# Latent attention: rows scaled before they are turned, and query and key heads made as features by tokens

## The chip, the cores and the metric

The kernel runs on one core of one Trainium2 chip. The metric is the device time of one execution in microseconds (us), measured over three runs; one more execution is profiled. The engines go by the profile's names: PE is TensorE's matmul, PEld its weight load, DVE VectorE, ACT ScalarE, POOL GpSimd, SP the engine that issues the loads of weights.

## What is computed

Two stacks of transformer blocks over 256 tokens with 1024 features, two layers each. The part that the change touches is the latent attention of the first stack, once a layer:

```python
def rmsnorm(x, g):
    y = xf * lax.rsqrt(jnp.mean(xf * xf, axis=-1, keepdims=True) + EPS)
    return (y * g.astype(jnp.float32)).astype(x.dtype)

# z = rmsnorm(x) @ w_in; c_q (256 x 384), c_kv (256 x 256), k_rope (256 x 64) are columns of z
def mla_attention(c_q, c_kv, k_rope, positions, norm_q, norm_kv, w_uq, w_ukv):
    q = (rmsnorm(c_q, norm_q) @ w_uq).reshape(bsz, seq, MLA_HEADS, QK_NOPE + QK_ROPE)
    kv = (rmsnorm(c_kv, norm_kv) @ w_ukv).reshape(bsz, seq, MLA_HEADS, QK_NOPE + V_DIM)
    q_nope, q_pe = q[..., :QK_NOPE], q[..., QK_NOPE:]
    k_nope, v = kv[..., :QK_NOPE], kv[..., QK_NOPE:]
    q_pe = apply_rope(q_pe, cos[:, :, None, :], sin[:, :, None, :])
    k_pe = apply_rope(k_rope, cos, sin)
    ...
        logits = (jnp.einsum('bqhd,bkhd->bhqk', qn, k_nope) + jnp.einsum('bqhr,bkr->bhqk', qp, k_pe)) * scale
        p = jax.nn.softmax(jnp.where(causal, logits, NEG_INF), axis=-1)
        return jnp.einsum('bhqk,bkhd->bqhd', p.astype(v.dtype), v)
```

There are 4 heads; QK_NOPE and V_DIM are 128, QK_ROPE is 64. The scores need queries and keys with the features on the partitions, the values with the tokens there.

## The kernel before

Tokens are two tiles (TT) of 128 rows, and a product contracts 128 features at a time on the partitions. Every weight product is made in three parts, from an upper and a lower half of each operand: `three` (line 517) multiplies upper by upper, upper by lower and lower by upper into one PSUM sum. In it a 128 x 128 tile of the activations is the stationary side and 512 (or 256) columns of weights the moving side, so the result has tokens on the partitions.

Weights stream through a ring of four chunks that SP loads (line 494). For each half chunk ACT makes the upper half (`cut`, line 2254) and DVE the lower one (line 1386). A cut may be made once PE has done with the half that lay in its slot; `half_used` tells that. Each engine has its own row of instructions, in the order of the program text of its function; semaphores alone tie them. PSUM has eight banks of 128 x 512; `free` and `held` make PE wait until a bank has been emptied.

The order in a layer around the change:

1. `project_in`: twelve blocks of z = h @ w_in, of which block 11 holds the latent columns c_q and c_kv (at Z_CQ and Z_CKV). ACT takes the squares of their rows behind block 4. Through the blocks DVE computes the 31 taps of a convolution (line 1721), the last of them in block 6; PE's matmuls of `mean` (line 844), in the last quarter of block 6, wait for tap 30.
2. `nsa_attention`: the latent rows are turned on PE in five tiles (`parts`, `part_group`, line 658: four tiles at once, one later) and cut into halves with the norm's weights (`c_hi`, `c_lo`). Then eight units of the sparse attention run in a loop: scores (952), softmax on DVE and ACT, transposes of the weights (693), ACT's copy (2399), values (709), DVE's gated output (1878) and POOL's sum over branches (2967). Between units stand other pieces: behind unit 1 DVE computes the mean squares of the latent rows, from which POOL makes the norm factors (`root`, line 2953); behind unit 4 PE makes the query product `uqn` (banks 0 and 1), behind unit 6 `uqp`. DVE scales these results by the norm factor as it empties them (1863).
3. `latent_attention`: PE makes `ukv`, key and value halves together, two halves of weights after each other. Behind the first half it turns the sparse attention's output (`nsaT`, line 658). ACT scales keys and values as it empties them (2370). PE turns the query heads (`qnT`) and starts the branch product `nsa0`; behind its first half it turns the key heads (`knT`) and then the rows that POOL has rotated (`rotT`, `kpT`; POOL's lines 2971 to 2987). Each turned pair of heads is copied from PSUM by DVE or ACT.
4. The latent attention's two units follow, among the rest of the branch products.

In the trace `ps` is PSUM, `z` the projections, `tT` and `nT` buffers of turned tiles, `ostage` the sparse attention's output, `st` the norm factors, `ring`, `upper_w` and `ring_lo` the weights with their two halves, `const` the identity for transposes. A helper's line stands for every caller.

## Time and profile before

| | us |
|---|---|
| median of three runs | 2070.93 |
| lowest, highest | 2070.07, 2073.01 |
| profiled execution, its own time | 2073.56 |
| its span, from first to last instruction | 2072.1 |
| PE busy in the span | 2044.6 |
| DVE busy | 1431.9 |
| ACT busy | 1180.3 |
| POOL busy | 65.8 |

Busy is the time in which an engine had at least one instruction under way. Matmuls overlap, so the duration of one matmul says little; the distance between the starts of two neighbours is what one costs. Where a row of the timeline stands for several instructions, its second column is the time from the first start to the last end. Idle time of an engine other than the one that bounds a stretch costs nothing by itself.

### The profile page before, as it was taken

To read this page: it belongs to the slowest core of one execution; us is meant where nothing else is said; L and a number is where in the kernel's file an instruction comes from. 1 tells how busy PE (TensorE), PEld (TensorE's weight loads), DVE (VectorE), ACT (ScalarE), POOL (GpSimd) and SP (SyncE) were. 2 spreads that over 40 slices of the span, in tenths; PEclk is the share of its full clock that TensorE was granted. 3 is DMA by queue.
4 is the path that set the end of the run, shared out by engine and by line. 5 is a ranking of instruction groups with operands and counts; after the bars stand their busy time and mean duration, and the time that the engine had idled before them with its cause. 6 is when DMAs were issued, how large, how long until landed. Compare 5 with 4: busy or idle time off the path is not lost.

```text
span 2072.1 us, 27212 instructions
## 1 busy us (share of the span) xinstructions
PE 2044.6 (99%) x10690; PEld 1723.7 (83%) x10690; DVE 1431.9 (69%) x2056; ACT 1180.3 (57%) x1906; POOL 65.8 (3%) x101
## 2 busy tenths in 40 slices
PE   9999999999999999999999999999999999999998
PEld 7877888888887788888888888878888888887887
DVE  6987756764698875676577557776765766587763
ACT  5547566553546656555465457755554655486552
POOL 0001100000000200000000000000000000010000
PEclk9999999999999999999999999999999999999999
DMA  7572344555555244455455554515555555545553
GB/s 251 198 247 100 144 164 149 191 196 183 186 202 213 92 163 158 154 198 183 183 203 193 185 212 183 214 68 195 185 184 200 186 192 186 203 151 192 186 199 123
DMA packets 54902, 372.56 MB, mean 180 GB/s; under 512 B 7471, under 2 KB 7767, under 8 KB 11128
## 3 DMA queue, kind: packets, MB, share of 16 engines
q1 hardware_dynamic: 49392, 356.54, 47.5%
q10 hardware_dynamic: 4872, 12.70, 1.9%
q0 software_dynamic: 512, 1.57, 0.3%
q8 instruction: 86, 1.41, 0.3%
q14 instruction: 40, 0.33, 0.0%
HBM read 369.46 MB, written 1.34 MB: 179 GB/s over the span
## 4 chain that ended last, share of the span: by engine, by line
PE 92%; ACT 3%; DVE 3%; DMA 1%; issue 1%; POOL 0%; SPq 0%; DVEq 0%; ACTq 0%; POOLq 0%
PE ps L567 21%; PE ps L519 17%; PE ps L523 17%; PE ps L520 17%; PE ps L573 11%; PE ps L709 1%; DMA ring<-in_w 1%; PE ps L602 1%; PE ps L642 1%; PE ps L658 1%; PE ps L693 1%; DVE ring_lo L1386 1%; ACT S L2392 1%; ACT upper_w L2254 0%; PE ps L1207 0%
## 5 line engine op out<-in xcount | busy, mean ns | idle before, releaser
L1386 DVE TENSOR_TENSOR ring_lo<-ring,upper_w 128x1024 fp32r<-128x1024 f32 x435 | 525.4, 1222 | 202.7 <-ACT upper_w L2254 201.6
L2254 ACT CAST upper_w<-ring 128x1024 fp32r<-128x1024 f32 x435 | 449.3, 1050 | 277.6 <-DMA ring<-in_w 163.3
L520 PE MATMUL ps<-ring_lo,nT_pair 128*128 128x512 f32 (+1 forms) x984 | 382.2, 388 | 0.0
L519 PE MATMUL ps<-upper_w,nT_pair 128*128 128x512 f32 (+1 forms) x848 | 337.4, 398 | 2.2 <-DVE ring_lo L1386 1.5
L523 PE MATMUL ps<-upper_w,nT_pair 128*128 128x512 f32 (+1 forms) x680 | 265.4, 390 | 0.0
L573 PEld LDWEIGHTS ps<-nT_pair,ring_lo 128*128 128x128 f32 x1920 | 246.2, 191 | 9.4
L573 PE MATMUL ps<-nT_pair,ring_lo 128*128 128x256 f32 x1920 | 249.0, 283 | 0.0
L520 PE MATMUL ps<-ring_lo,z_hi 128*128 128x512 f32 x624 | 242.9, 389 | 0.0
L567 PE MATMUL ps<-nT_pair,upper_w 128*128 128x512 f32 x960 | 230.0, 391 | 0.0
L520 PEld LDWEIGHTS ps<-ring_lo,nT_pair 128*128 128x128 f32 x984 | 185.6, 189 | 35.3
L567 PEld LDWEIGHTS ps<-nT_pair,upper_w 128*128 128x128 f32 x960 | 176.5, 188 | 34.2
L523 PE MATMUL ps<-upper_w,tT_lo 128*128 128x512 f32 (+1 forms) x528 | 204.8, 388 | 0.0
L519 PEld LDWEIGHTS ps<-upper_w,nT_pair 128*128 128x128 f32 x848 | 159.9, 189 | 38.6 <-issue 3.5
L1386 DVE TENSOR_TENSOR ring_lo<-ring,PT_w 128x1024 fp32r<-128x1024 f32 x112 | 134.9, 1220 | 55.2 <-ACT PT_w L2254 55.2
L1386 DVE TENSOR_TENSOR ring_lo<-ring,S_w 128x1024 fp32r<-128x1024 f32 x112 | 134.7, 1219 | 46.5 <-ACT S_w L2254 46.5
L2254 ACT CAST PT_w<-ring 128x1024 fp32r<-128x1024 f32 x112 | 115.5, 1050 | 70.0 <-DMA ring<-in_w 70.0
L2456 ACT COPY z<-ps 128x512 f32<-128x512 f32 x60 | 35.2, 587 | 207.6 <-PE ps L573 207.6
L523 PEld LDWEIGHTS ps<-upper_w,nT_pair 128*128 128x128 f32 x680 | 127.9, 188 | 27.3 <-DVE nT_pair L1448 0.7
L1618 DVE TENSOR_TENSOR acc<-ps,z 128x512 f32<-128x512 f32 x60 | 41.5, 692 | 156.0 <-ACT z L2456 156.0
L2254 ACT CAST S_w<-ring 128x1024 fp32r<-128x1024 f32 x112 | 115.5, 1050 | 55.8 <-DMA ring<-in_w 55.6
L519 PE MATMUL ps<-upper_w,z_hi 128*128 128x512 f32 x360 | 142.1, 395 | 0.0
L520 PEld LDWEIGHTS ps<-ring_lo,z_hi 128*128 128x128 f32 x624 | 117.3, 188 | 23.4
(389 smaller groups left out, 2876.7 us busy)
## 6 DMA issues: line engine op xcount, KB each, us to landing
ring<-in_w SPq DMA_DIRECT2D x338, 1024.0 KB, 4.8
big<-in_gains ACTq DMA_DIRECT2D x7, 512.0 KB, 4.2
z<-in_mem ACTq DMA_DIRECT2D x2, 1024.0 KB, 7.5
big<-skew POOLq DMA_DIRECT2D x8, 192.0 KB, 6.7
x<-in_x SPq DMA_DIRECT2D x2, 512.0 KB, 7.4
ring<-in_w SPq DMA_DIRECT2D x2, 512.0 KB, 7.0
PTs<-skew ACTq DMA_DIRECT2D x1, 1024.0 KB, 4.6
big<-skew ACTq DMA_DIRECT2D x1, 1024.0 KB, 8.8
```

The costliest lines, as they stand in the source:

```text
L519: PE.matmul(out, hi, w_hi, start=start, stop=False)
L520: PE.matmul(out, hi, w_lo, start=False, stop=False)
L523: return PE.matmul(out, lo, w_hi, start=False, stop=stop)
L567: PE.matmul(ps[:, base + i, :], upper(W.halves[h][2])[:, cols], nT_pair[:, :, 2 * c + k, :], start=(c == 0 and k == 0), stop=False)
L573: m = PE.matmul(ps[:, base + i, 0:T], w_lo[:, cols], nT_hi[:, 2 * c + k, :], start=False, stop=(2 * c + k == KT - 1))
L602: m = PE.transpose(ps[:, b, i * P:(i + 1) * P], src[:, t, (4 * g + i) * P:(4 * g + i + 1) * P], ident)
L642: m = PE.transpose(ps[:, b, (i * TT + t) * P:(i * TT + t + 1) * P], src(c + i, t), ident)
L658: m = PE.transpose(ps[:, b, (i * TT + t) * P:(i * TT + t + 1) * P], src(c + i, t), ident)
L1386: V.tensor_tensor(ring_lo[:, q % RING, cols], ring[:, q % RING, cols], upper(n).bitcast(F32), ALU.subtract).then_inc(*lo_cut.up(h))
L1618: V.tensor_tensor(pair(b), ps[:, base:base + 2, 0:T], ffn_half[:, 0:2, :], ALU.add).then_inc(*dve_out.up())
L2254: A.copy(upper(n), ring[:, q % RING, part * HALF:(part + 1) * HALF]).then_inc(*hi_cut.up(h))
L2456: A.copy(ffn_half[:, 0:2, :], ps[:, base:base + 2, T:2 * T]).then_inc(*act_out.up(f"{f}.hg{b}"))
```

## The change

The mean squares of the latent rows move from the loop of the sparse attention into block 6 of `project_in`. POOL, once it has both norm factors, multiplies the latent columns of z by them in place, in four instructions, and PE's turns of these columns wait for that. The gains of the norm stay where they were, in the cut behind the turn.

A new helper `three_turned` exchanges the sides of the three products: 128 columns of weights are stationary, and the 256 tokens of a turned tile are the moving side, so the result has the features of one head on the partitions. The query product `uqn` and the key half of `ukv` are made so, head by head, each over all of its row blocks; both halves of the weights are awaited before the first matmul. Their results are copied once, without a factor, into the places that the turned heads had. The turns `qnT` and `knT` go. The value half of `ukv` is made as before, behind the key half, and the turn `nsaT` stands behind the first half of the value product. Values and rotary queries are copied without a factor.

```diff
...
+        def three_turned(out, hi, lo, w_hi, w_lo, start, stop):
+            PE.matmul(out, w_hi, hi, start=start, stop=False)
+            PE.matmul(out, w_hi, lo, start=False, stop=False)
+            return PE.matmul(out, w_lo, hi, start=False, stop=stop)
         def gemm(seg, lhs, banks, ready=(), beside=None, first=0, kts=None, width=BLK):
...
         def nsa_attention(l):
-            c_at = parts(f"{l}.c", cols_of(z, Z_CQ), 4, lambda c: (), (6, 7))
+            c_at = parts(f"{l}.c", cols_of(z, Z_CQ), 4, lambda c: [pool_out.at(f"{l}.latents")], (6, 7))
...
-            beside = {4: lambda: latent_queries(f"{l}.uqn", 512, (0, 1), f"{l}.qn"), 6: lambda: latent_queries(f"{l}.uqp", 256, (2, 3), f"{l}.qp")}
+            def latent_heads():
+                free(0, 1)
+                w = [weights(h) for h in W.span[f"{l}.uqn"]]
+                for n in range(4):
+                    for k in range(3):
+                        w_hi, w_lo = w[k // 2]
+                        if n == 0:
+                            PE.wait_ge(*c_at[k])
+                        cols = slice(k % 2 * BLK + n * P, k % 2 * BLK + (n + 1) * P)
+                        m = three_turned(ps[:, n // 2, n % 2 * T:(n % 2 + 1) * T], c_hi(k), c_lo(k), w_hi[:, cols], w_lo[:, cols], k == 0, k == 2)
+                        if n == 3 and k:
+                            m.then_inc(*half_used.up(W.span[f"{l}.uqn"][k - 1]))
+                held(dve_out.at(f"{l}.qnT"), 0, 1)
+            beside = {4: latent_heads, 6: lambda: latent_queries(f"{l}.uqp", 256, (2, 3), f"{l}.qp")}
             attention(nsa_units(l), scores, lambda i: [act_out.at(f"{l}.k.0"), act_out.at(f"{l}.q.2")] if i == 0 else (), first=conv_product, beside=beside, by_act=True,
...
             PE.wait_ge(*dve_out.at(f"{l}.c.lo4"))
+            w = [weights(h) for h in W.span[f"{l}.ukv"]]
+            for n in range(4):
+                for k in range(2):
+                    w_hi, w_lo = w[k]
+                    cols = slice(n * P, (n + 1) * P)
+                    m = three_turned(ps[:, 4 + n // 2, n % 2 * T:(n % 2 + 1) * T], c_hi(3 + k), c_lo(3 + k), w_hi[:, cols], w_lo[:, cols], k == 0, k == 1)
+            m.then_inc(*psum_full.up(f"{l}.knT"))
             for k, h in enumerate(W.span[f"{l}.ukv"]):
-                w_hi, w_lo = weights(h)
-                for hf, b in ((0, 4), (1, 0)):
-                    for t in range(TT):
-                        cols = slice(hf * BLK, (hf + 1) * BLK)
-                        m = three(ps[:, b + t, :], c_hi(3 + k, TOK[t]), c_lo(3 + k, TOK[t]), w_hi[:, cols], w_lo[:, cols], k == 0, k == 1)
+                w_hi, w_lo = w[k]
+                for t in range(TT):
+                    m = three(ps[:, t, :], c_hi(3 + k, TOK[t]), c_lo(3 + k, TOK[t]), w_hi[:, BLK:2 * BLK], w_lo[:, BLK:2 * BLK], k == 0, k == 1)
                 m.then_inc(*half_used.up(h))
...
                     parts(f"{l}.nsaT", cols_of(ostage), 4, lambda c: [pool_out.at(f"{l}.nsa7.sum")], (6, 7))
-            held(act_out.at(f"{l}.kn"), 4, 5)
+            held(dve_out.at(f"{l}.knT"), 4)
+            held(act_out.at(f"{l}.knT"), 5)
             held(act_out.at(f"{l}.vn"), 0, 1)
-            turn(f"{l}.qnT", cols_of(z, QN), 4, [dve_out.at(f"{l}.qn")], split_evac(f"{l}.qnT"), banks=(2, 3))
...
                 if c == 0:
-                    turn(f"{l}.knT", cols_of(z, KN), 4, [act_out.at(f"{l}.kn")], split_evac(f"{l}.knT"), banks=(4, 5))
                     turn(f"{l}.rotT", lambda c, t: rot[:, t, 2 * c:2 * c + 2, :].rearrange("p h r -> p (h r)"), 2, [pool_out.at(f"{l}.rot")], split_evac(f"{l}.rotT"), banks=(0, 1))
...
-            work = {0: lambda: (tap(28), block_keys()), 1: lambda: (tap(29), tap(30), block_scores(), centre()), 3: lambda: (deviation(), block_weights())}
+            work = {0: lambda: (mean_square(f"{l}.cq", TT, Q_RANK, 4), mean_square(f"{l}.ckv", TT, KV_RANK, 6), tap(28), block_keys()), 1: lambda: (tap(29), tap(30), block_scores(), centre()), 3: lambda: (deviation(), block_weights())}
             cuts(f"{l}.in6", lambda n: work.get(n, lambda: None)())
...
-            def squares():
-                cut_ahead(W.span[f"{l}.conv0"][1])
-                mean_square(f"{l}.cq", TT, Q_RANK, 4)
-                mean_square(f"{l}.ckv", TT, KV_RANK, 6)
-            def queries(n, width, at, bank):
-                V.wait_ge(*product(f"{l}.u{n}"))
-                for t in range(TT):
-                    V.tensor_scalar(z[:, t, at:at + width], ps[:, bank + t, 0:width], st[:, 4 + t:5 + t], None, ALU.mult).then_inc(*dve_out.up(f"{l}.{n}" if t else None))
-            def latent_queries():
-                V.wait_ge(*pool_out.at(f"{l}.cq.rstd"))
-                queries("qn", 512, QN, 0)
+            def latent_heads():
+                V.wait_ge(*product(f"{l}.uqn"))
+                V.tensor_copy(tT[:, 0:4, :], ps[:, 0:2, :].rearrange("p b (c n) -> p (b c) n", n=T)).then_inc(*dve_out.up(f"{l}.qnT"))
                 cuts(f"{l}.uqp")
...
             lo_group(f"{l}.c", 5, 4, *c_parts, sm[:, S1["mq"][0]:S1["mkv"][1]], (6, 7))
-            attention(units, out, first=lambda: cut_ahead(W.span[f"{l}.conv0"][0]), by_act=True, beside={1: squares, 2: lambda: cut_ahead(W.span[f"{l}.conv1"][0]),
-                      3: lambda: cut_ahead(W.span[f"{l}.conv1"][1]), 5: lambda: cuts(f"{l}.uqn"), 6: latent_queries}, between=conv_product, second=second_product)
-            queries("qp", 256, QP, 2)
+            attention(units, out, first=lambda: cut_ahead(W.span[f"{l}.conv0"][0]), by_act=True, beside={1: lambda: cut_ahead(W.span[f"{l}.conv0"][1]), 2: lambda: cut_ahead(W.span[f"{l}.conv1"][0]),
+                      3: lambda: cut_ahead(W.span[f"{l}.conv1"][1]), 5: lambda: cuts(f"{l}.uqn"), 6: latent_heads}, between=conv_product, second=second_product)
+            V.wait_ge(*product(f"{l}.uqp"))
+            V.tensor_copy(z[:, :, QP:QP + 256], ps[:, 2:4, 0:256]).then_inc(*dve_out.up(f"{l}.qp"))
...
             lo_parts(f"{l}.nsaT", 4, of_parts(nsa_parts), banks=(6, 7))
-            pair_to(f"{l}.qnT", 0, tT, 2)
+            V.wait_ge(*psum_full.at(f"{l}.knT"))
+            V.tensor_copy(tT[:, 9:11, :], ps[:, 4, :].rearrange("p (c n) -> p c n", n=T)).then_inc(*dve_out.up(f"{l}.knT"))
...
                 if n == 0:
-                    pair_to(f"{l}.knT", 0, tT[:, 9:13, :], 4)
                     pair_to(f"{l}.rotT", 0, tT[:, 13:15, :], 0)
...
             hi_parts(f"{l}.nsaT", 4, of_parts(nsa_parts)[0], banks=(6, 7))
-            A.wait_ge(*pool_out.at(f"{l}.ckv.rstd"))
+            A.wait_ge(*psum_full.at(f"{l}.knT"))
+            A.copy(tT[:, 11:13, :], ps[:, 5, :].rearrange("p (c n) -> p c n", n=T)).then_inc(*act_out.up(f"{l}.knT"))
             A.wait_ge(*product(f"{l}.ukv"))
-            scaled(f"{l}.kn", z[:, :, KN:KN + 512], ps[:, 4:6, :], 6)
-            scaled(f"{l}.vn012", z[:, :, VN[0]:VN[0] + 3 * P], ps[:, 0:2, 0:3 * P], 6)
-            scaled(f"{l}.vn", z[:, :, VN[3]:VN[3] + P], ps[:, 0:2, 3 * P:4 * P], 6)
-            pair_to(f"{l}.qnT", 2, tT[:, 2:4, :], 3)
+            A.copy(z[:, :, VN[0]:VN[0] + 3 * P], ps[:, 0:2, 0:3 * P]).then_inc(*act_out.up())
+            A.copy(z[:, :, VN[3]:VN[3] + P], ps[:, 0:2, 3 * P:4 * P]).then_inc(*act_out.up(f"{l}.vn"))
...
                 if n == 0:
-                    pair_to(f"{l}.knT", 2, tT[:, 11:13, :], 5)
                     A.wait_ge(*psum_full.at(f"{l}.kpT.0"))
...
             root(f"{l}.ckv", TT, 6, f"{l}.ckv.rstd")
+            G.wait_ge(*pool_out.at(f"{l}.ckv.rstd"))
+            for t in range(TT):
+                for at, rank, i in ((Z_CQ, Q_RANK, 4 + t), (Z_CKV, KV_RANK, 6 + t)):
+                    rows_ = z[:, t, at:at + rank]
+                    G.tensor_scalar(rows_, rows_, st[:, i:i + 1], None, ALU.mult).then_inc(*pool_out.up(f"{l}.latents" if t and at == Z_CKV else None))
             sums(l)
...```

PE in the latent stage, at the end of the first half of the branch product `nsa0` (`z_hi` holds its left side). Before:

```order
L519 MATMUL ps<-upper_w,z_hi 128x512
L520 MATMUL ps<-ring_lo,z_hi 128x512
L523 MATMUL ps<-upper_w,z_hi 128x512
L642 MATMUL ps<-const,z 128x128 x8
L642 MATMUL ps<-const,tT 128x128 x6
```

After:

```order
L519 MATMUL ps<-upper_w,z_hi 128x512
L520 MATMUL ps<-ring_lo,z_hi 128x512
L523 MATMUL ps<-upper_w,z_hi 128x512
L648 MATMUL ps<-const,tT 128x128 x6
L519 MATMUL ps<-upper_w,z_hi 128x512
```

The eight turns of key heads are gone, and the six of the rows that POOL rotated follow directly on the product.

DVE in block 6 (line 1386, after the change 1410, is the cut of weights; 1721, then 1745, a tap for one of four channel tiles). Before:

```order
L1386 TENSOR_TENSOR ring_lo<-ring,upper_w 128x1024 x2
L1721 SCALAR_TENSOR_TENSOR acc<-cbuf,sm,acc 128x256 x4
L1783 COPY kcz<-ps 64x15
L1784 COPY kcz<-ps 64x15
L1386 TENSOR_TENSOR ring_lo<-ring,upper_w 128x1024
L1721 SCALAR_TENSOR_TENSOR acc<-cbuf,sm,acc 128x256 x8
```

After:

```order
L1410 TENSOR_TENSOR ring_lo<-ring,upper_w 128x1024 x2
L1461 TENSOR_SCALAR st<-st 128x2 x2
L1745 SCALAR_TENSOR_TENSOR acc<-cbuf,sm,acc 128x256 x4
L1807 COPY kcz<-ps 64x15
L1808 COPY kcz<-ps 64x15
L1410 TENSOR_TENSOR ring_lo<-ring,upper_w 128x1024
L1745 SCALAR_TENSOR_TENSOR acc<-cbuf,sm,acc 128x256 x8
```

The two mean squares stand ahead of the last twelve tap instructions.

POOL in layer 0, from its last load of the bias band to the rotation. Before:

```order
L3000 DMA big<-skew 16x8x384 x8
L2953 TENSOR_TENSOR st<-st,half 128x2 x2
L2967 TENSOR_TENSOR ostage<-ostage,acc 128x256 x8
L2971 COPY z<-z 128x2x64
L2979 TENSOR_TENSOR tT<-z,rope 128x5x32
```

After:

```order
L3013 DMA big<-skew 16x8x384 x8
L2966 TENSOR_TENSOR st<-st,half 128x2 x2
L3020 TENSOR_SCALAR z<-z,st 128x384
L3020 TENSOR_SCALAR z<-z,st 128x256
L3020 TENSOR_SCALAR z<-z,st 128x384
L3020 TENSOR_SCALAR z<-z,st 128x256
L2980 TENSOR_TENSOR ostage<-ostage,acc 128x256 x8
L2984 COPY z<-z 128x2x64
```

Four scalings in place stand between the roots and the first sum of the sparse attention.

## Rows read from the trace of the kernel before

**Rows 1.** The page, its first part: busy time, share, instructions.

```profile
PE 2044.6 (99%) x10690; PEld 1723.7 (83%) x10690; DVE 1431.9 (69%) x2056; ACT 1180.3 (57%) x1906; POOL 65.8 (3%) x101
```

**Rows 2.** Timeline of PE, layer 0: start, us, line, operation, tiles, count, [idle before].

```profile
199.33 0.39 PE L520 MATMUL ps<-ring_lo,nT_pair 128*128 128x512 f32 x1
...
202.98 0.39 PE L523 MATMUL ps<-upper_w,tT_lo 128*128 128x512 f32 x1
203.21 1.03 PE L693 MATMUL ps<-const,S 128*128 128x128 f32 x8
...
205.94 1.06 PE L693 MATMUL ps<-const,S 128*128 128x128 f32 x8 [0.85 <-ACT PTs L2399]
...
208.75 0.28 PE L520 MATMUL ps<-ring_lo,nT_pair 128*128 128x256 f32 x1
...
210.65 0.28 PE L523 MATMUL ps<-upper_w,tT_lo 128*128 128x256 f32 x1
...
212.48 0.47 PE L519 MATMUL ps<-upper_w,nT_pair 128*128 128x512 f32 x1
...
215.33 1.04 PE L658 MATMUL ps<-const,ostage 128*128 128x128 f32 x8
...
218.97 1.03 PE L642 MATMUL ps<-const,z 128*128 128x128 f32 x8
219.76 0.48 PE L519 MATMUL ps<-upper_w,z_hi 128*128 128x512 f32 x1
...
223.46 0.82 PE L642 MATMUL ps<-const,tT 128*128 128x128 f32 x6
```

**Rows 3.** Timeline of DVE, POOL and ACT in the sparse attention's loop, layer 0.

```profile
191.77 0.23 DVE L1437 TENSOR_SCALAR st<-st 128x2 f32<-128x2 f32 x2
192.02 1.38 POOL L2953 TENSOR_TENSOR st<-st,half 128x2 f32<-128x2 f32 x2 [62.58 <-DVE st L1437]
194.37 0.42 DVE L1878 TENSOR_TENSOR acc<-ps,fac 128x256 f32<-128x256 f32 x1 [0.73 <-POOL ostage L2967]
204.80 0.99 ACT L2399 COPY PTs<-ps 128x1024 f32<-128x1024 f32 x1
```

**Rows 4.** Timeline of DVE and POOL in the latent stage, layer 0.

```profile
216.62 1.44 DVE L1386 TENSOR_TENSOR ring_lo<-ring,upper_w 128x1024 fp32r<-128x1024 f32 x1 [1.37 <-ACT upper_w L2254]
216.93 1.51 POOL L2982 TENSOR_TENSOR tT<-z,rope 128x160 f32<-128x160 f32 x1
217.98 1.40 DVE L1425 TENSOR_TENSOR z_hi<-ps,z_hi 128x256 fp32r<-128x256 f32 x4
223.06 0.24 POOL L2987 COPY tT<-tT 128x64 f32<-128x64 f32 x1
```

**Rows 5.** Timeline of DVE and PE in block 6, layer 0, then layer 1.

```profile
144.39 3.25 DVE L1721 SCALAR_TENSOR_TENSOR acc<-cbuf,sm,acc 128x256 f32<-128x256 f32 x8
149.19 1.89 PE L844 MATMUL ps<-acc,const 128*128 128x256 f32 x8
651.04 3.25 DVE L1721 SCALAR_TENSOR_TENSOR acc<-cbuf,sm,acc 128x256 f32<-128x256 f32 x8
654.60 1.89 PE L844 MATMUL ps<-acc,const 128*128 128x256 f32 x8
672.02 1.04 PE L658 MATMUL ps<-const,z 128*128 128x128 f32 x8
```

**Rows 6.** Timeline of DVE and POOL in the recurrent part: taps alone, taps beside scalings.

```profile
1821.17 2.96 DVE L2142 SCALAR_TENSOR_TENSOR tT<-big,sm,tT 128x256 f32<-128x256 f32 x6
1830.76 3.18 DVE L2142 SCALAR_TENSOR_TENSOR tT<-big,sm,tT 128x256 f32<-128x256 f32 x6 [3.23 <-POOL tT L3024]
1830.17 2.98 POOL L3024 TENSOR_SCALAR tT<-big,sm 128x256 f32<-128x256 f32 x4 [11.37 <-ACT big L2380]
```

**Rows 7.** Timeline of PE, then a window: busy of five engines, granted clock, DMA.

```profile
139.18 0.60 PE L898 MATMUL ps<-hidT,sm 128*128 128x30 f32 x4 [1.78 <-ACT hidT L2561]
...
140.00:143.40 3.40, 3.40 (x13) 2.62 (x11) 3.31 (x8) 2.38 (x6) 0.00 (x0) 0.50 1.02 419
```

## The prediction

> **What bounds the kernel now.** The page first: TensorE (PE) is busy 99% of the span [rows 1]. So a change is worth what it takes from PE's row of instructions, less what PE then waits for. The second view is PE's timeline in the latent stage of layer 0, 199 to 224 us [rows 2]; layer 1 repeats it. The reader is to see two things there: the starts of consecutive matmuls, which give the price of one slot, and that PE waits once in the stretch, 0.85 us at 205.94. The third view is the timeline of VectorE (DVE), ScalarE (ACT) and GpSimd (POOL) behind that wait and beside the turns [rows 3, 4]: who would be late next. The fourth is the stretch in block 6 of the input projection, where the change puts its new work [rows 5].
>
> **Slots.** Between 199.33 and 202.98 lie 16 slots of the query product, 512 columns each: 3.65 / 16 = 0.228 us. Between 208.75 and 210.65 lie 16 slots of 256 columns: 1.90 / 16 = 0.119 us [rows 2]. Half the columns cost a little over half, although each brings its own weight load.
>
> **Query product.** Before 18 slots of 512: 18 x 0.228 = 4.10 us. After 36 of 256 (4 heads, 3 row blocks, 3 products): 36 x 0.119 = 4.28. More by 0.18 a layer. It ends just ahead of the 0.85 us wait, which ends with an ACT copy that began at 204.80 [rows 2, 3]; the 0.18 fits in it and costs nothing there. Without that cover it costs 0.18.
>
> **Key half of the ukv product.** Before 12 x 0.228 = 2.74, after 24 x 0.119 = 2.86: more by 0.12. The value half keeps its 12 slots.
>
> **Turns that go.** The query heads' eight transposes take 219.76 - 218.97 = 0.79 [rows 2]; the key heads' eight are the same again, together 1.58 us a layer. PE's own work falls by 1.58 - 0.12 - 0.18 = 1.28 a layer, 2.56 in all. That is not yet the gain.
>
> **The 0.85 us wait.** In the loop of the sparse attention DVE does two mean squares (0.23 together), POOL two roots after them (1.38), and POOL's first head sums queue behind the roots; DVE's output at 194.37 then waits 0.73 for such a sum [rows 3]. All four instructions leave the loop. DVE's row could so run up to 0.73 + 0.23 = 0.96 earlier, and with it the exponentials and ACT's copy of 204.80. The copy can't start before the end of the transposes it reads, 203.21 + 1.03 = 204.24 [rows 2], and after the change 0.18 later, 204.42. I take 204.80 - 204.42 = 0.38 less a hand-over, so 0.35 us a layer. The bounds are 0 (another wait holds DVE) and 0.85.
>
> **First new wait: the sparse attention's rows.** Their turn (nsaT) starts at 215.33; the first lower part is ready a quarter of 1.40 after 217.98, at 218.33, so 3.00 us later; PE asks for it at 219.76, 4.43 after the start, with 1.43 to spare [rows 2, 4]. What covered it was half of ukv (12 slots) and the query turn. After the change only six value slots stand there: 0.79 for the turn, 6 x 0.228 + 0.10 for the restart = 1.47, so PE asks after 2.26. Ahead of the lower parts DVE still has a weight cut, which waits for a slot that the first ukv half frees, also just ahead of this turn; so the 3.00 hold. PE waits 3.00 - 2.26 = 0.74 us, and 0.5 if the cut is not stretched to 1.44 as in its row [rows 4].
>
> **Second new wait: the rotated rows.** POOL ends the rotation at 223.06 + 0.24 = 223.30; PE reaches their turn at 223.46, with 0.16 to spare [rows 2, 4]. POOL's chain starts at the output of the last sparse unit, which moves with PE, so it ends 0.35 earlier, at 222.95. PE starts the branch product at 212.48 - 0.35 + 2.86 + 1.47 + 0.79 + 1.47 + 0.74 = 219.46, and after 12 slots and a restart (2.84) is at the turn at 222.30: it waits 0.65. So POOL decides this stage. Whatever PE saves ahead of the turn, it goes on at 222.95 where it went on at 223.46: **0.51 us a layer**, the 0.16 and the 0.35. Bounds: 0.16, if POOL's chain doesn't move, and 1.58 - 0.12 + 0.35 = 1.81, if neither new wait forms, since POOL's 1.51 [rows 4] shows how much a DVE cut beside it can stretch one of its instructions, and it may be spared.
>
> **What moves into block 6.** DVE gets the two mean squares (0.23 [rows 3]) ahead of the taps, POOL two roots and four scalings in place. The scaled rows are needed by the c turns. In layer 1 the taps behind the mean squares end at 651.04 + 3.25 = 654.29, and the c turns come at 672.02: some 17 us for POOL's work of about 5. The turns wait for nothing. But the taps gate PE's mean product at 654.60, 0.31 after their end; in layer 0 the gap is 149.19 - 147.64 = 1.55 [rows 5]. How much POOL slows the taps is not in this stretch. The nearest row is the recurrent part, where six taps beside four such scalings take 3.18 instead of 2.96 [rows 6]: 0.22 / 4 = 0.055 an instruction, and for six 0.33. So DVE is late by 0.23 + 0.33 = 0.56: PE waits **0.25 us** in layer 1 and not in layer 0. Bounds: 0, and the whole of POOL's time (rival B).
>
> A rule of the Trainium skill speaks against this place. The page SBUF — State Buffer, section Who interferes with whom, says that an instruction of DVE with two SBUF inputs and one of GpSimd that reads SBUF exclude each other, and that the later one blocks in full. The taps have two SBUF inputs. By the rule taken at its word they would lose whole scalings, and the sum would be that of rival B; the row, 0.22 us lost beside 2.98 us of POOL, shows DVE losing little [rows 6]. The stretch of POOL's 1.51 agrees with the other side of it [rows 4].
>
> **The rest.** ACT's and DVE's scaled evacuations become plain copies, fewer in number, in rows that do not hold PE; ACT's go under PE's branch product. No DMA is added or moved.
>
> **Sum.** -0.51 x 2 + 0.25 = -0.77 us. The profiled execution took 2073.56: 2072.79. The median of the three timed runs is 2070.93, 2.63 below the profiled one; the difference carries over, so I predict **2070.2 us**.
>
> **Rivals.** A: the new waits don't form, since POOL's chain and the lower parts get as much earlier as PE. For it: the stretched 1.51 on POOL and 1.44 on DVE can both vanish. Against it: the spare of 0.16 is small. It gives -1.81 x 2 + 0.25 = -3.37: 2067.6. Chance 0.20.
>
> B, slower: POOL holds DVE for whole instructions in block 6. Two roots (1.38), two scalings of 256 columns at 2.98 / 4 = 0.745 and two of 384 at 1.12 [rows 3, 6] are 5.1 us; with 0.23 and less the spare, layer 0 loses 3.8 and layer 1 5.0, less the 1.0 of the latent stages: +7.8, 2078.7. If DVE is held for x us a layer, the loss is 2x - 1.4; it outweighs the 1.0 from x = 1.2 on, and the sum is over 0.2% from 3.3 on. Against it: rows 6. Chance 0.04.
>
> C: the two waits lower TensorE's clock. After a wait of 1.78 us at 139.18 the granted clock is 0.50, 1.2 GHz, from 140.0 to 143.4 [rows 7]: 3.4 us do the work of 1.7. Twice this, 3.4 - 0.8 = +2.6: 2073.5. Against it: the forecast's waits are 0.74 and 0.65, with 2.8 us of work between them. Chance 0.10.
>
> **How the numbers follow.** Forecast 0.66, A 0.20, C 0.10, B 0.04. The three timed runs span 2.94 us, so about 0.2%, 4.1 us, is what a measurement can tell from no change. Faster than 2066.8 needs A and a little more: 0.05. Slower than 2075.1 needs B, or C with more: 0.05. The same: 0.90. The range reaches below to A, 2067.2. Above it takes in the forecast's worse bounds (2070.93 - 2 x 0.16 + 1.0 with DVE 1.3 late in layer 1, 2071.6) and the smaller half of C (one lowered clock, 2071.9), with about 1 us for the scatter of a median: 2072.9.
>
> **What would show it.** Right: PE's query product some 4.3 us long, the 0.85 us wait about halved, two new PE waits, one for DVE's lower part ahead of the branch product and one for POOL's rotation, each 0.4 to 0.9, in both layers; PE's mean product in layer 1 waiting about 0.25 for the taps. Wrong: 256-column slots over 0.13 us with weights as the stationary side; PE going on at the rotary turn more than 1 us or less than 0.2 us earlier; taps of block 6 slowed by more than 1 us; a c turn that waits for POOL; a granted clock of 0.50 in this stage.

## The result and the profile after

| | before | after |
|---|---|---|
| median, us (20 runs each) | 2071.45 | 2075.11 |
| lowest, highest, us | 2069.54, 2074.49 | 2072.76, 2077.45 |
| profiled execution: time, span, us | 2073.56, 2072.1 | 2074.47, 2073.0 |

The ratio of the times is 1.0018, with a 95% interval of 1.0011 to 1.0025: the changed kernel is slower by 3.7 us, and the prediction (2070.2, 2067.2 to 2072.9) was wrong in sign and range. In all figures below one execution of 9513 us, of the kernel with the late rotary turn, is left out. PE's busy time fell by 2.2 us [rows 1]; more than that came back as waits, and some of it as a lowered clock, which counts as busy. The page of the kernel after, first part:

```profile
PE 2042.4 (99%) x10718; PEld 1721.9 (83%) x10718; DVE 1432.6 (69%) x2050; ACT 1176.1 (57%) x1896; POOL 80.7 (4%) x109
```

The timeline of PE in the latent stage of layer 0 after the change, against [rows 2] (start, us, line, operation, tiles, count, [idle before, releaser]):

```profile
196.92 0.36 PE L527 MATMUL ps<-nT_pair,upper_w 128*128 128x256 f32 x1
...
201.31 1.04 PE L699 MATMUL ps<-const,S 128*128 128x128 f32 x8
...
203.54 1.06 PE L699 MATMUL ps<-const,S 128*128 128x128 f32 x8 [0.35 <-ACT PTs L2414]
...
214.44 1.03 PE L664 MATMUL ps<-const,ostage 128*128 128x128 f32 x8
...
218.67 0.47 PE L519 MATMUL ps<-upper_w,z_hi 128*128 128x512 f32 x1 [1.80 <-DVE z_hi L1449]
...
220.56 0.63 PE L519 MATMUL ps<-upper_w,z_hi 128*128 128x512 f32 x1
...
221.84 0.63 PE L519 MATMUL ps<-upper_w,z_hi 128*128 128x512 f32 x1
...
223.07 0.82 PE L648 MATMUL ps<-const,tT 128*128 128x128 f32 x6
```

The query product takes 201.31 - 196.92 = 4.39, the 0.85 us wait has become 0.35, and the new wait ahead of the branch product is 1.80 where 0.74 was forecast. Behind it three slots take 221.84 - 220.56 = 1.28, so 0.43 each instead of 0.23. Windows of the same kernel show why (us, then busy of PE, PEld, DVE, ACT and POOL, the granted clock, DMA): half the clock, 1.2 GHz, in layer 0, and full clock behind the same wait in layer 1.

```profile
220.00:221.00 1.00, 1.00 (x4) 0.71 (x4) 0.47 (x1) 0.00 (x0) 1.00 (x2) 0.50 0.91 385
221.00:222.00 1.00, 1.00 (x4) 0.81 (x3) 0.00 (x0) 0.00 (x0) 0.58 (x2) 0.50 0.03 8
...
727.00:728.00 1.00, 1.00 (x6) 0.84 (x5) 0.95 (x2) 0.14 (x1) 0.92 (x2) 1.00 0.97 410
728.00:729.00 1.00, 1.00 (x7) 0.81 (x6) 0.44 (x1) 0.00 (x0) 1.00 (x2) 1.00 0.90 369
```

DVE, POOL and ACT in that stage, layer 0, against [rows 4]. The last of the four lower parts (L1449) ends at 217.16 + 1.41 = 218.57, and PE goes on 0.10 later. Two instructions of POOL's rotation are stretched, 1.11 and 1.38 long, where before there was one; each ends just behind a weight cut of DVE (L1410). The last row is ACT's cast, the upper half that the cut at 219.21 needs:

```profile
215.72 1.52 DVE L1410 TENSOR_TENSOR ring_lo<-ring,upper_w 128x1024 fp32r<-128x1024 f32 x1 [2.87 <-ACT upper_w L2269]
217.16 1.41 DVE L1449 TENSOR_TENSOR z_hi<-ps,z_hi 128x256 fp32r<-128x256 f32 x4
...
219.21 1.26 DVE L1410 TENSOR_TENSOR ring_lo<-ring,upper_w 128x1024 fp32r<-128x1024 f32 x1
...
216.22 1.11 POOL L3000 COPY tT<-tT 128x64 f32<-128x64 f32 x1
...
219.47 1.38 POOL L2997 TENSOR_TENSOR tT<-tT 128x160 f32<-128x160 f32 x1
...
221.40 0.24 POOL L3000 COPY tT<-tT 128x64 f32<-128x64 f32 x1
...
218.07 1.11 ACT L2269 CAST upper_w<-ring 128x1024 fp32r<-128x1024 f32 x1
```

POOL's chain now ends 221.64 - 203.54 = 18.10 behind the start of PE's turn of softmax weights; before it was 223.30 - 205.94 = 17.36 [rows 2, 4]. The cut at 219.21 is 15.67 behind the same start; before it was 17.47 behind it (223.41), just past the chain's end. There it waited 3.11 for ACT, whose cast followed six scaled evacuations and a copy in ACT's row. These rows of the kernel before:

```profile
219.23 2.72 ACT L2370 ACTIVATE z<-ps,st 128x512 f32<-128x512 f32 x6 [1.56 <-PE ps L523]
...
222.28 1.10 ACT L2254 CAST upper_w<-ring 128x1024 fp32r<-128x1024 f32 x1
...
223.41 1.23 DVE L1386 TENSOR_TENSOR ring_lo<-ring,upper_w 128x1024 fp32r<-128x1024 f32 x1 [3.11 <-ACT upper_w L2254]
```

Block 6 after the change, against [rows 5]: the taps are slowed in both layers, and PE's mean product now waits in both.

```profile
143.01 3.94 DVE L1745 SCALAR_TENSOR_TENSOR acc<-cbuf,sm,acc 128x256 f32<-128x256 f32 x8
147.01 1.99 PE L850 MATMUL ps<-acc,const 128*128 128x256 f32 x8 [0.49 <-DVE acc L1745]
...
649.59 1.48 DVE L1410 TENSOR_TENSOR ring_lo<-ring,upper_w 128x1024 fp32r<-128x1024 f32 x1
650.99 3.93 DVE L1745 SCALAR_TENSOR_TENSOR acc<-cbuf,sm,acc 128x256 f32<-128x256 f32 x8
654.98 1.99 PE L850 MATMUL ps<-acc,const 128*128 128x256 f32 x8 [0.48 <-DVE acc L1745]
...
649.41 5.29 POOL L3020 TENSOR_SCALAR z<-z,st 128x384 f32<-128x384 f32 x4
```

To sum by stage, four landmarks of PE in layer 1: the block keys' product, the mean product, and two turns of softmax weights, and at the end the rotary turn. First the rows of before (that of the mean product is in [rows 5]), then of after:

```profile
650.05 1.91 PE L915 MATMUL ps<-kcz,tT 128*128 128x32 f32 x16
...
708.62 1.03 PE L693 MATMUL ps<-const,S 128*128 128x128 f32 x8
...
711.32 1.06 PE L693 MATMUL ps<-const,S 128*128 128x128 f32 x8 [0.82 <-ACT PTs L2399]
...
728.81 0.82 PE L642 MATMUL ps<-const,tT 128*128 128x128 f32 x6
```

```profile
649.71 1.94 PE L921 MATMUL ps<-kcz,tT 128*128 128x32 f32 x16
...
709.28 1.04 PE L699 MATMUL ps<-const,S 128*128 128x128 f32 x8
...
711.51 1.06 PE L699 MATMUL ps<-const,S 128*128 128x128 f32 x8 [0.35 <-ACT PTs L2414]
...
729.66 0.87 PE L648 MATMUL ps<-const,tT 128*128 128x128 f32 x6
```

| stretch, layer 1 | before | after | difference | forecast |
|---|---|---|---|---|
| block keys to mean product (taps) | 4.55 | 5.27 | +0.72 | +0.25 |
| to the turn ahead of the 0.85 us wait (query product) | 54.02 | 54.30 | +0.28 | +0.18 |
| over that wait | 2.70 | 2.23 | -0.47 | -0.53 |
| to the rotary turn | 17.49 | 18.15 | +0.66 | -0.16 |

That is +1.19 in layer 1. Layer 0 has nearly the same first three (+0.78, +0.28, -0.50), and 2.01 in the last (205.94 to 223.46 before, 203.54 to 223.07 after), of which 2.01 - 0.66 = 1.35 is put down to the lowered clock. Together that is 3.8 us for this one pair of executions; the medians differ by 3.7. Outside the table, the block keys' product itself waits 0.22 us for DVE in layer 0; the kernels below without the mean squares ahead of the taps show no such wait for DVE.

The two profiled executions differ by only 0.9 us, because the one of before held a disturbance that the one of after lacks: the 1.78 us wait and the lowered clock at 139 to 143 [rows 7]. At the block keys' product of layer 0 the one of before stands at 144.68, the one of after at 141.72, 2.96 earlier. In the same place the kernel after ran at full clock:

```profile
140.00:143.40 3.40, 3.18 (x23) 2.63 (x21) 3.31 (x7) 2.61 (x7) 3.29 (x4) 1.00 1.06 378
```

### The profile page after: what moved, and what is told of

Read it like the earlier page. It is cut to its first block, busy times and chain, and to the rows that moved or that the text cites. A ratio compares the mean times of both kernels' runs of the same rounds, so it can differ in the third digit from the quotient of the medians.

```text
span 2073.0 us, 27254 instructions
## 1 busy us (share of the span) xinstructions
PE 2042.4 (99%) x10718; PEld 1721.9 (83%) x10718; DVE 1432.6 (69%) x2050; ACT 1176.1 (57%) x1896; POOL 80.7 (4%) x109
## 3 DMA queue, kind: packets, MB, share of 16 engines
q8 instruction: 86, 1.41, 0.3%
## 4 chain that ended last, share of the span: by engine, by line
PE 91%; ACT 3%; DVE 3%; DMA 1%; POOL 0%; issue 0%; SPq 0%; DVEq 0%; ACTq 0%
PE ps L573 21%; PE ps L519 17%; PE ps L523 16%; PE ps L520 16%; PE ps L579 11%; PE ps L715 2%; DMA ring<-in_w 1%; PE ps L608 1%; PE ps L699 1%; PE ps L648 1%; DVE ring_lo L1410 1%; PE ps L664 1%; ACT upper_w L2269 1%; DVE acc L1745 1%; PE ps L958 0%
## 5 line engine op out<-in xcount | busy, mean ns | idle before, releaser
L1410 DVE TENSOR_TENSOR ring_lo<-ring,upper_w 128x1024 fp32r<-128x1024 f32 x435 | 526.5, 1224 | 202.3 <-ACT upper_w L2269 200.8
L2269 ACT CAST upper_w<-ring 128x1024 fp32r<-128x1024 f32 x435 | 449.4, 1050 | 282.3 <-DMA ring<-in_w 165.8
L520 PE MATMUL ps<-ring_lo,nT_pair 128*128 128x512 f32 (+2 forms) x964 | 374.1, 388 | 0.0
L519 PE MATMUL ps<-upper_w,nT_pair 128*128 128x512 f32 (+2 forms) x828 | 328.5, 397 | 3.0 <-DVE ring_lo L1410 2.2
L523 PE MATMUL ps<-upper_w,nT_pair 128*128 128x512 f32 (+1 forms) x680 | 264.9, 390 | 0.0
L520 PE MATMUL ps<-ring_lo,z_hi 128*128 128x512 f32 x624 | 243.6, 390 | 0.0
L520 PEld LDWEIGHTS ps<-ring_lo,nT_pair 128*128 128x128 f32 x964 | 181.4, 188 | 34.5
L523 PE MATMUL ps<-upper_w,tT_lo 128*128 128x512 f32 (+1 forms) x508 | 197.1, 388 | 0.0
L519 PEld LDWEIGHTS ps<-upper_w,nT_pair 128*128 128x128 f32 x828 | 155.8, 188 | 38.4 <-issue 4.1
L1410 DVE TENSOR_TENSOR ring_lo<-ring,PT_w 128x1024 fp32r<-128x1024 f32 x112 | 135.0, 1221 | 55.1 <-ACT PT_w L2269 55.1
L1410 DVE TENSOR_TENSOR ring_lo<-ring,S_w 128x1024 fp32r<-128x1024 f32 x112 | 134.8, 1219 | 45.5 <-ACT S_w L2269 45.5
L2269 ACT CAST PT_w<-ring 128x1024 fp32r<-128x1024 f32 x112 | 115.5, 1050 | 69.8 <-DMA ring<-in_w 69.7
L523 PEld LDWEIGHTS ps<-upper_w,nT_pair 128*128 128x128 f32 x680 | 127.6, 188 | 27.2 <-DVE nT_pair L1472 0.7
L2269 ACT CAST S_w<-ring 128x1024 fp32r<-128x1024 f32 x112 | 115.4, 1049 | 54.8 <-DMA ring<-in_w 54.7
L519 PE MATMUL ps<-upper_w,z_hi 128*128 128x512 f32 x360 | 142.6, 396 | 3.6 <-DVE z_hi L1449 3.6
L520 PEld LDWEIGHTS ps<-ring_lo,z_hi 128*128 128x128 f32 x624 | 117.5, 188 | 23.5
```

The source lines that it names most:

```text
L519: PE.matmul(out, hi, w_hi, start=start, stop=False)
L520: PE.matmul(out, hi, w_lo, start=False, stop=False)
L523: return PE.matmul(out, lo, w_hi, start=False, stop=stop)
L1410: V.tensor_tensor(ring_lo[:, q % RING, cols], ring[:, q % RING, cols], upper(n).bitcast(F32), ALU.subtract).then_inc(*lo_cut.up(h))
L2269: A.copy(upper(n), ring[:, q % RING, part * HALF:(part + 1) * HALF]).then_inc(*hi_cut.up(h))
```

## The experiments

Each was timed beside runs of the kernel before on the same chip; differences are to the median of these.

**The two parts alone.** First the kernel before with the scaled rows only (a scaling in block 6, plain copies, no other product or turn changed).

```diff
-            work = {0: lambda: (tap(28), block_keys()), 1: ...
+            work = {0: lambda: (mean_square(f"{l}.cq", TT, Q_RANK, 4), mean_square(f"{l}.ckv", TT, KV_RANK, 6), tap(28), block_keys()), 1: ...
...
+                    G.tensor_scalar(rows_, rows_, st[:, i:i + 1], None, ALU.mult).then_inc(...)
```

> The kernel before with one part of the change: mean squares, roots and scalings in block 6, plain copies behind; products and turns as before. Theory: block 6 costs 0.77 a layer, the wait of 0.85 us at the transposes falls to 0.35, and nothing else changes: (0.77 - 0.5) x 2 = 0.5 above before. Rival: the scaled rows alone carry the loss, 3 us or more above before.

Measured: 2073.35, ratio 1.0012 (1.0003 to 1.0021), 2.3 above before. Neither number was right. In layer 1 block 6 cost about what was expected (0.72), and 0.46 was saved at the loop's wait, but 0.80 was lost from there to the rotary turn. PE (first row) waits there for POOL, and POOL's last copy of 0.24 us has met a weight cut and takes 1.11:

```profile
731.40 0.87 PE L642 MATMUL ps<-const,tT 128*128 128x128 f32 x6 [0.61 <-POOL tT L2983]
...
730.23 1.11 POOL L2983 COPY tT<-tT 128x64 f32<-128x64 f32 x1
...
729.79 1.46 DVE L1386 TENSOR_TENSOR ring_lo<-ring,upper_w 128x1024 fp32r<-128x1024 f32 x1 [2.33 <-ACT upper_w L2251]
```

Then the heads alone, with the mean squares and the roots back in the loop; the norm factor of the latent rows is left out of this kernel:

```diff
-            c_at = parts(f"{l}.c", cols_of(z, Z_CQ), 4, lambda c: [pool_out.at(f"{l}.latents")], (6, 7))
+            c_at = parts(f"{l}.c", cols_of(z, Z_CQ), 4, lambda c: (), (6, 7))
...
-                    G.tensor_scalar(rows_, rows_, st[:, i:i + 1], None, ALU.mult).then_inc(...)
```

> The kernel after with the other part alone: heads made as features, no turns of them, but the mean squares and roots in the loop as before and no scaling; the norm factor of the latent rows is left out of the computation. Theory: block 6 is as before; the query product's 0.29 more fits under the wait at the transposes (0.85 falls to about 0.55); the latent stage loses 0.66 a layer to the 1.80 us wait ahead of nsa0 and to POOL's rotation, and about 1.4 more in a layer whose clock falls after that wait: 1.3 to 4 above before, with one lowered clock 2.7. Rival: without the scalings the turns that went show as a gain, 1 below before.

Measured: 2073.84, ratio 1.0011 (1.0002 to 1.0020), 2.8 above before, as expected with one lowered clock (2.7): the turns that went are no gain by themselves. The 1.80 us wait is there in both layers, and this time the clock fell in layer 1 only. This kernel also has block 6 as before without the disturbance of [rows 7], and shows what the slack in layer 0 is there: DVE's taps end at 145.70, PE's mean product starts at 146.04.

```profile
142.45 3.25 DVE L1745 SCALAR_TENSOR_TENSOR acc<-cbuf,sm,acc 128x256 f32<-128x256 f32 x8
...
146.04 1.89 PE L850 MATMUL ps<-acc,const 128*128 128x256 f32 x8
```

**Block 6.** The mean squares behind the taps:

```diff
-            work = {0: lambda: (mean_square(f"{l}.cq", ...), mean_square(f"{l}.ckv", ...), tap(28), block_keys()), 1: lambda: (tap(29), tap(30), block_scores(), centre()), ...
+            work = {0: lambda: (tap(28), block_keys()), 1: lambda: (tap(29), tap(30), block_scores(), centre(), mean_square(f"{l}.cq", ...), mean_square(f"{l}.ckv", ...)), ...
```

> The kernel after, with the two mean squares of block 6 behind DVE's centring of the convolution in place of ahead of the last twelve taps, so that POOL's roots and scalings run after the taps. Theory: PE's wait for the taps (0.48 in both layers, and DVE 1.08 later than before) goes: 0.77 a layer, 1.5 below the kernel after, 2.2 above before; POOL ends some 9 us ahead of the turns of the latent rows. Rival 1: the wait is of the two mean squares on DVE's row alone (0.14); then 0.3 comes back. Rival 2: the scalings now slow the work behind the taps by as much, and nothing comes back.

Measured: 2074.04, ratio 1.0013 (1.0004 to 1.0022), 2.2 above before, the number of the theory. PE's wait for the taps is gone, but rival 2 came in part: in layer 0 DVE's four copies of the block weights take 0.92 beside the scalings in place of 0.48, and PE waits 0.65 for them where it waited 0.23 in the kernel after; in layer 1 it waits 0.27. The second kernel of the pair keeps DVE's row and moves POOL alone:

```diff
+            G.wait_ge(*dve_out.at(f"{l}.tap30.3"))
             root(f"{l}.cq", TT, 4, f"{l}.cq.rstd")
```

> The kernel after; the mean squares stay ahead of the taps, but POOL's roots and scalings wait for the last tap. It tells POOL's slowing from the mean squares' own place in DVE's row. Theory: of DVE's 1.08 us nearly all is POOL (taps 3.93 in place of 3.25, a weight cut 1.48 in place of 1.23), and 0.14 is the mean squares: the taps go back to 3.25, PE's wait of 0.48 goes, and the time comes 1.5 below the kernel after, 2.2 above before, as with the mean squares behind the taps. Rival: the mean squares' place is the cause; then the wait stays at 0.4 or more and the time at that of the kernel after.

Measured: 2073.41, ratio 1.0009 (1.0000 to 1.0018), 2.4 above before. The mean squares are still ahead of the taps, and these are back to their old time:

```profile
647.29 0.23 DVE L1461 TENSOR_SCALAR st<-st 128x2 f32<-128x2 f32 x2
...
649.53 1.23 DVE L1410 TENSOR_TENSOR ring_lo<-ring,upper_w 128x1024 fp32r<-128x1024 f32 x1
650.67 3.25 DVE L1745 SCALAR_TENSOR_TENSOR acc<-cbuf,sm,acc 128x256 f32<-128x256 f32 x8
```

So POOL's scalings are the cause of the longer taps and of PE's wait behind them (block keys to mean product take 4.63 here, 5.27 in the kernel after, 4.55 before): 3.93 - 3.25 = 0.68 on eight taps and 1.48 - 1.23 = 0.25 on the weight cut, 0.93 for four scalings.

**The wait ahead of the branch product, and what stands beside it.** The turn nsaT in other banks of PSUM:

```diff
-                    parts(f"{l}.nsaT", cols_of(ostage), 4, lambda c: [pool_out.at(f"{l}.nsa7.sum")], (6, 7))
+                    parts(f"{l}.nsaT", cols_of(ostage), 4, lambda c: [pool_out.at(f"{l}.nsa7.sum")], (2, 3))
...
-            lo_parts(f"{l}.nsaT", 4, of_parts(nsa_parts), banks=(6, 7))
+            lo_parts(f"{l}.nsaT", 4, of_parts(nsa_parts), banks=(2, 3))
```

> The kernel after, with the turn nsaT in PSUM banks 2 and 3 (free there) in place of 6 and 7, the banks that the branch product nsa0 writes. Theory: PE's 1.80 us wait ahead of nsa0 is the release of the two banks by the last of the four lower parts, three parts of 0.35 later than the first one; with other banks PE asks for the first part alone and waits 1.80 - 1.05 = 0.75. But POOL's rotation ends when it did (its end was 0.03 ahead of the next matmul in layer 1), so PE then waits about 1.1 at the turn rotT, and the time stays within 0.4 us of the kernel after, 3.3 to 3.7 above the kernel before; 1.4 less where the lowered clock of layer 0 goes with the long wait. Rival 1: the parts themselves are late (behind DVE's weight cut); then the wait stays at 1.8. Rival 2: POOL's rotation doesn't hold PE; then all of 1.05 a layer comes back, 1.6 above before.

Measured: 2074.34, ratio 1.0011 (1.0002 to 1.0020), 2.5 above before. The list of PE's waits (us in total, times, longest) has the first wait at 0.9 instead of 1.8, and a second one of 1.0 where there had been 0.2:

```profile
PE ps L648 <- POOL tT L3000: 2.0, 2, 1.0
PE ps L519 <- DVE z_hi L1449: 1.7, 2, 0.9
```

The release of the banks is the cause of the long wait, and POOL takes over what is saved. The 1.1 us below the kernel after is about what the lowered clock had cost; it stayed up in both layers here. Next the rotary turn behind the second half of the branch product, first without, then with the other banks:

```diff
             def rotated(c):
-                if c == 0:
+                if c == 1:
```

> The kernel after, with the turns rotT and kpT (and their copies) behind the second half of nsa0 in place of the first. Theory: the 1.80 us wait ahead of nsa0 is still there and hides nearly all of POOL's lateness; only the 0.2 us wait at rotT in layer 1 goes. Time 0.2 to 0.4 below the kernel after, so 3.3 to 3.5 above before. Rival: what PE pays in this stage is POOL's rotation, and the wait ahead of nsa0 is only where it shows; then about 1 us a layer comes back, 1.7 above before.

Measured: ratio 1.0025 (1.0014 to 1.0036), so some 5.2 us above before; worse than either theory had it. The 1.80 us wait stays, the clock fell in both layers, and a wait that nobody expected of this kernel comes up at the first scores, which now follow the rotary turn with nothing between:

```profile
728.33 0.47 PE L519 MATMUL ps<-upper_w,z_hi 128*128 128x512 f32 x1 [1.81 <-DVE z_hi L1449]
...
737.35 0.68 PE L1047 MATMUL ps<-tT 128*128 128x128 f32 x4 [1.05 <-ACT nT L2653]
```

> Both edits: nsaT in banks 2 and 3, rotT and kpT behind the second half of nsa0. Theory of two waits side by side: neither edit alone gives much, both together give 1.05 + 0.2 a layer in layer 1 and 1.05 in layer 0, 2.3 below the kernel after, 1.4 above before; 1.4 less again where the clock of layer 0 stays up, so about level with before. PE's wait ahead of nsa0 0.75, none at rotT. Rival: the turned rows then come late for the scores of the first latent unit, and the gain is taken back there.

Measured: 2074.34, ratio 1.0012 (1.0003 to 1.0020), 2.5 above before. The rival came: in both layers the wait ahead of the product is 0.85, that for POOL is gone, and the first scores wait 1.05 for the turned rows' copies, so nothing is won over the banks alone.

The last of this group takes the kernel with the other banks and moves one weight cut of DVE behind POOL's chain:

```diff
-            cuts(f"{l}.nsa0", rotated)
+            rotated(0)
+            cuts(f"{l}.nsa0")
```

> The kernel with nsaT in banks 2 and 3 (where PE waits 1.0 us at rotT for POOL's rotation), with one edit on DVE alone: the copy of rotT stands ahead of the weight cut of nsa1's second half, so that this cut falls behind POOL's chain. Theory: a POOL instruction that meets a weight cut on DVE waits for the cut's end, which made one of 0.53 us last 1.39; without the meeting POOL's chain ends 0.86 earlier, PE's wait at rotT falls to about 0.15, and the time is 1.7 below the kernel with the banks alone, 0.8 to 1.0 above the kernel before. Rival: POOL's chain is long for another reason (its own order, or ACT's copies in the same stretch); then its end and PE's wait stay.

Measured: 2071.88, ratio 1.0003 (0.9994 to 1.0011), 0.3 above before and 2.2 better against it than the banks alone. No POOL instruction of the second half of the chain is stretched any more (the one of 1.39 us is 0.53 again, as the timeline shows), and PE's wait for POOL, 1.0 with the banks alone, is 0.2 at most in the list of waits:

```profile
727.06 0.53 POOL L2998 TENSOR_TENSOR tT<-tT 128x160 f32<-128x160 f32 x1
```

```profile
PE ps L648 <- POOL tT L3001: 0.3, 2, 0.2
```

**Versions of the changed kernel with the waits covered.** The first has the other banks; the halves of nsaT cut ahead of the weights of nsa1; POOL's copy of the rotary key columns taken out of its chain; the rotary turn at three quarters of the product; the mean squares behind the taps:

```diff
-            cuts(f"{l}.ukv")
-            lo_parts(f"{l}.nsaT", 4, of_parts(nsa_parts), banks=(6, 7))
+            cut_ahead(W.span[f"{l}.ukv"][0])
+            lo_parts(f"{l}.nsaT", 4, of_parts(nsa_parts), banks=(2, 3))
+            cut_ahead(W.span[f"{l}.ukv"][1])
...
-            gemm(f"{l}.nsa0", ..., rotated)
+            gemm(f"{l}.nsa0", ..., amid={2: rotated})
```

> The kernel after with five moves of order: nsaT turned into banks 2 and 3; the halves of its rows cut ahead of the weights of nsa1; POOL's copy of the rotary key columns taken out of its chain behind the sparse attention and put behind the scalings; rotT and kpT turned at three quarters of nsa0; the mean squares behind the taps. Theory (three waits side by side: lower parts, POOL's rotation, the turned rows for the first scores): with all of them covered PE waits nowhere between the turn nsaT and the first scores, some 2.0 us a layer less than the kernel after, 0.77 a layer less in block 6, and no lowered clock in layer 0 for want of a wait: 5.5 to 6.5 below the kernel after, 1.8 to 2.8 below the kernel before. Rival: what PE saves is given back at the softmax of the first latent unit, where DVE and ACT are next; then it stays within 1 us of the kernel before.

Measured: 2071.27, ratio 1.0000 (0.9991 to 1.0009), 0.2 above before; the expectation was missed by 2 us or more, and only in small part for the rival's reason. Two waits were left: for POOL at the rotary turn, since its rotation now met three weight cuts on its way, and at the turn of the block weights, since the scalings now ran beside DVE's copies of these weights:

```profile
728.05 0.87 PE L650 MATMUL ps<-const,tT 128*128 128x128 f32 x6 [0.66 <-POOL tT L3002]
...
663.26 0.66 PE L932 MATMUL ps<-const,tT 128*128 128x128 f32 x4 [0.65 <-DVE tT L1833]
...
737.50 0.66 PE L701 MATMUL ps<-const,S 128*128 128x128 f32 x4 [0.28 <-ACT S L2409]
```

The last row is the rival's place, the softmax weights of the first latent unit, where PE did not wait before. The second version takes these away:

```diff
+            G.wait_ge(*dve_out.at(f"{l}.tap30.3"))
...
-            cuts(f"{l}.nsa0", rotated)
+            rotated(0)
+            cuts(f"{l}.nsa0")
...
-            merge(f"{l}.nsap0", 1, 0, ps[:, 6:8, :], f"{l}.nsag0")
+            V.tensor_tensor(first_half, ps[:, 6:8, :], first_half, ALU.mult).then_inc(*dve_out.up(f"{l}.nsap0"))
...
+            attention(mla_units(l), plain_out, ..., between=first_sum)
```

> The version with five moves of order, with three edits: the mean squares stand ahead of the taps again and POOL waits for the last tap (in the earlier version DVE's work behind the taps met the scalings, and PE waited 0.43 us longer at the turn of the block weights); rotT's copy stands ahead of the weight cut of nsa1's second half on DVE, as in the other kernel of this set (PE waited 0.66 at rotT for POOL); and DVE adds the first product of nsa to the merged rows behind its scores of the first latent unit in place of ahead of them. Theory: 0.43 and 0.66 a layer go, 2.2 in all, and the softmax of the first latent unit doesn't take them back, since DVE has 1.2 us less ahead of it: 2.0 below the kernel before. Rival: DVE and ACT are the bound from the end of nsa0 to the turns of the first unit's weights, and the 0.66 returns there as a longer wait: 0.7 below before.

Measured: 2068.41, ratio 0.9986 (0.9977 to 0.9995): 3.1 below before, the only kernel of the study that beats it. PE runs from the turn of nsaT to the first scores without a wait (timeline, layer 1), busy throughout at full clock (window):

```profile
719.13 1.04 PE L666 MATMUL ps<-const,ostage 128*128 128x128 f32 x8
...
725.48 0.81 PE L650 MATMUL ps<-const,tT 128*128 128x128 f32 x6
...
727.52 0.60 PE L1048 MATMUL ps<-tT 128*128 128x128 f32 x4
```

```profile
720.00:728.00 8.00, 8.00 (x42) 6.66 (x40) 5.35 (x8) 5.93 (x12) 4.95 (x9) 1.00 0.40 131
```

None of the three waits of the first version stands in this profile beyond the 0.2 us at the block weights that the kernel before has too. How the three edits share the gain over the first version was not tried one by one.

## Why the prediction was wrong, point by point

The sum took its 0.51 us a layer from one step: "Whatever PE saves ahead of the turn, it goes on at 222.95", where POOL ends, 0.35 earlier than before. This step failed. From the query product to the rotary turn PE came out 0.28 - 0.47 + 0.66 = 0.47 later in layer 1 in place of 0.51 earlier. Both things that the step rests on were wrong, PE's own way to the turn (first new wait) and the end of POOL's chain (second new wait), and each was nearly enough for this loss. Two of the prediction's signs of being wrong came with it: PE is not even 0.2 us earlier at the rotary turn, and the granted clock is 0.50 in this stage.

**Slots, query product, turns: right.** 4.39 us for 4.28 (the first slot of another shape starts 0.1 later), the key half 2.95 for 2.86, and the turns are gone.

**The 0.85 us wait: right in mechanism.** It fell to 0.35. Net of the longer product 0.2 a layer was won where 0.35 was forecast.

**First new wait: mis-sized, 1.80 for 0.74.** The prediction let PE go on at the first lower part, "a quarter of 1.40 after 217.98". But the branch product writes the PSUM banks (6 and 7) in which the turned rows lie, and `free` lets it start when the fourth part has left them, 3 x 0.35 = 1.05 later: 0.74 + 1.05 = 1.8, what the trace shows. The other banks brought it to 0.85. The trace of before could have said so: there too the product (219.76) started behind the fourth part (217.98 + 1.40 = 219.38) [rows 2, 4]; the spare was 0.4, not 1.43.

**Second new wait: right that POOL decides, wrong that its chain moves with PE.** The chain starts with PE's last sparse unit, as forecast, but it ends 18.10 - 17.36 = 0.74 later against PE than before, since it meets one weight cut more: the cut of nsa1's second half, which fell behind the chain before, comes 17.47 - 15.67 = 1.80 earlier against PE and falls on it now. The prediction had read POOL's 1.51 as a stretch that "may be spared" and did not ask which other cuts would move onto the chain. What moved this one is in the part that it put at nothing, the evacuations that become plain copies "in rows that do not hold PE". ACT's row held the cut; with fewer and shorter copies in it the cast comes 218.07 - 203.54 = 14.53 behind that start in place of 222.28 - 205.94 = 16.34. With it the cut comes earlier; the cut now holds POOL, and POOL holds PE. ACT's share is read from the rows; no run changed ACT alone. With the cut behind the chain the wait went.

In the kernel after, the two new waits lie over each other: PE pays the longer one, and in layer 1 the turn at 729.66 goes on where POOL ends. So the banks alone won nothing but the clock. The later turn alone left the 1.80 us wait and added one of 1.05 at the first scores.

**Block 6: the term was mis-sized, twice.** POOL's slowing was taken from [rows 6] as 0.055 a scaling and measured 0.93 / 4 = 0.23: the weight cut ahead of the taps was left out, and the recurrent taps were no fair stand-in. And the slack of 1.55 in layer 0 [rows 5] was not slack of the kernel: PE was late there by the disturbance of [rows 7]. Undisturbed it is 0.34, close to the 0.31 of layer 1. So both layers lose 0.7 to 0.8, where 0.25 in one was forecast.

**The profiled execution against the median.** That "the difference carries over" was wrong: the profiled execution of the kernel after lies 0.6 below its median. The 2.63 is about what the disturbance of [rows 7] cost (2.96 at the block keys' product), seen there and yet taken as a constant. The number did not suffer, since 0.77 below the median of 2070.93 is 2070.2 without it too; the slack of layer 0 did.

**Rival C came in half.** The clock fell behind the 1.80 us wait in one layer of the kernel after, for 1.35 us; the rival had 1.7 in each of two. Over the five kernels that keep this wait (after, the late squares, the late rotary turn, POOL's wait, the heads alone) the profiles show it in five layers of ten; in the kernels with 0.85 there or none, in no layer of ten. Why it falls in one layer and not in the other stays open; no run here tests it.

**Rival B and the rule behind it.** The taps were not held for whole instructions. By the rule of the Trainium skill named in the prediction (SBUF — State Buffer, Who interferes with whom) the loss would have been that of whole scalings; here DVE lost 0.23 a scaling. In POOL's direction the trace agrees with the rule: a rotation that meets a weight cut ends only behind it.

## What to carry to other kernels

When cover is taken from in front of a product, ask what releases it by everything that it writes as well as by what it reads: a bank that still holds its own input turns "first part ready" into "last part read". When a chain on a slow engine becomes the bound, list which instructions of its neighbours will fall on it after the move, not only before it; here each weight cut that fell on it cost 0.9 us. A row that holds nobody up can still hold such an instruction back, as ACT's did here. And before a slack or a difference to the median is used as a constant, look whether the stretch it was read in was undisturbed in the other layer.

## What the runs showed of the hardware that was not expected

A POOL instruction that reads SBUF and meets DVE's subtraction of two SBUF tiles (1.22 us) ends about 0.1 to 0.4 behind that subtraction: 0.53 became 1.33 to 1.53, 0.24 became 1.11, while the same instructions beside the lower parts, which take one input from PSUM, kept 0.53. The subtraction itself grew where a POOL instruction was under way at its start, the more of it was left: in layer 0 of the kernel after from 1.22 to 1.52 with 0.43 us left, and to 1.26 with 0.18 left. Where DVE runs taps of 0.4 us, the loss is shared: POOL's four scalings took 5.29 (4.28 with the mean squares late), and the eight taps beside them 3.93 in place of 3.25.

A lowered clock after a wait of PE is not certain: after 1.8 us it came five times in ten, each time for 3.4 us at 0.50. In the three kernels that have it in one layer of two (after, POOL's wait, the heads alone), that layer took 1.3 us more from the start of the branch product to the first scores than the other. With the late rotary turn this stretch took 1.6 more than in the kernel that has the other banks as well, where the clock stayed up. At the place of [rows 7] it came after 1.78 us in the kernel before, but not after 2.80 in the kernel with the scaled rows alone, nor after 1.62 in the second version with the waits covered.
